# Second layer's attention: 50 joined steps for 80

## The reference

```
s_c = einsum(qc, k_cmp) * scale;  p_c = masked_softmax(s_c, cmp_end <= qpos);  o_c = p_c @ v_cmp    # 31 blocks
s_s = einsum(qr, k_sel) * scale;  p_s = masked_softmax(s_s, tok_pos <= qpos);  o_s = p_s @ v_sel
s_w = einsum(qr, kw_i) * scale;   p_w = masked_softmax(s_w, mask_w);           o_w = p_w @ vw_i
o = gi[..., 0:1] * o_c + gi[..., 1:2] * o_s + gi[..., 2:3] * o_w
```

## Time and profile before

| | |
|---|---|
| median of 3 runs | 3423.38 us (3423.05 to 3425.78) |
| profiled execution | 3428.43 us |
| its span | 3426.1 us |
| PE busy | 3238.9 us |
| DVE, ACT, POOL busy | 1606.8, 1433.4, 1603.5 us |
| second layer's attention, first score phase to the last value phase | 803.54 to 969.23 us |

### The profile page before, as it was taken

How to read it: one execution, slowest core, us unless ns; L and a number is a source line. 1 busy time by engine, 2 the same in 40 slices (tenths; PEclk the granted TensorE clock), 3 DMA queues, 4 the chain that set the end, 5 groups by cost and what they waited for, 6 DMA issues and landing times.

```text
span 3426.1 us, 45293 instructions
## 1 busy us (share of the span) xinstructions
PE 3238.9 (95%) x16790; PEld 2643.6 (77%) x16790; DVE 1606.8 (47%) x2363; ACT 1433.4 (42%) x2565; POOL 1603.5 (47%) x1403
## 2 busy tenths in 40 slices
PE   6789999999999999999989986999999999999998
PEld 4567888876578888788867774888888888888887
DVE  4783443135733431444157875555565562234421
ACT  3355333325753333433245554444454532243332
POOL 4245444655554447444543321444444435554454
PEclk8889999998999999999999997999999999999999
DMA  4111333341013333333321220111111113333332
GB/s 119 50 44 50 98 98 94 97 126 49 2 55 97 94 93 101 88 98 95 97 79 50 62 56 25 32 38 38 38 38 38 44 45 98 98 96 94 98 92 80
DMA packets 471624, 246.88 MB, mean 72 GB/s; under 512 B 13883, under 2 KB 468774, under 8 KB 471334
## 3 DMA queue, kind: packets, MB, share of 16 engines
q1 hardware_dynamic: 470144, 241.33, 24.9%
q10 hardware_dynamic: 1318, 3.35, 0.3%
HBM read 241.51 MB, written 2.10 MB: 71 GB/s over the span
## 4 chain that ended last, share of the span: by engine, by line
PE 84%; DVE 8%; ACT 4%; issue 3%; POOL 1%; DMA 0%; POOLq 0%; ACTq 0%; DVEq 0%
PE ps L466 18%; PE ps L468 18%; PE ps L467 18%; PE ps L2346 2%; PE ps L2242 2%; PE ps L2244 2%; PE ps L2243 2%; PE ps L1573 2%; PE ps L2328 2%; PE ps L1583 2%; PE ps L1596 1%; PE ps L1761 1%; PE ps L1762 1%; PE ps L1763 1%; PE ps L1834 1%
## 5 line engine op out<-in xcount | busy, mean ns | idle before, releaser
L448 POOL TENSOR_TENSOR w_lo<-ring,w_hi 128x512 fp32r<-128x512 f32 (+1 forms) x908 | 1228.1, 1374 | 1543.0 <-ACT w_hi L439 1543.0
L439 ACT ACTIVATE w_hi<-ring 128x512 fp32r<-128x512 f32 (+1 forms) x908 | 516.1, 617 | 1271.6 <-PE ps L468 1199.8
L466 PE MATMUL ps<-h_hi,w_hi 128*128 128x512 f32 x1776 | 701.8, 395 | 4.4 <-POOL w_lo L448 4.4
L468 PE MATMUL ps<-h_hi,w_lo 128*128 128x512 f32 x1776 | 692.6, 390 | 0.0
L467 PE MATMUL ps<-h_lo,w_hi 128*128 128x512 f32 x1640 | 639.3, 390 | 0.0
L466 PEld LDWEIGHTS ps<-h_hi,w_hi 128*128 128x128 f32 x1776 | 334.2, 188 | 81.0 <-POOL w_lo L448 6.4
L468 PEld LDWEIGHTS ps<-h_hi,w_lo 128*128 128x128 f32 x1776 | 333.9, 188 | 69.8
L467 PEld LDWEIGHTS ps<-h_lo,w_hi 128*128 128x128 f32 x1640 | 308.7, 188 | 68.3 <-issue 4.6
L467 PE MATMUL ps<-a_lo,w_hi 128*128 128x512 f32 x752 | 292.6, 389 | 0.0
L466 PE MATMUL ps<-a_hi,w_hi 128*128 128x512 f32 x720 | 280.8, 390 | 0.0
L468 PE MATMUL ps<-a_hi,w_lo 128*128 128x512 f32 x720 | 280.2, 389 | 0.0
(11 more groups left out here) (454 smaller groups left out, 5745.2 us busy)
## 6 DMA issues: line engine op xcount, KB each, us to landing
ring<-in_ffn_w_in SPq DMA_DIRECT2D x176, 512.0 KB, 3.8
ring<-in_w_in SPq DMA_DIRECT2D x96, 512.0 KB, 4.0
ring<-in_ffn_w_down SPq DMA_DIRECT2D x32, 512.0 KB, 3.9
ring<-in_ffn_w_out SPq DMA_DIRECT2D x32, 512.0 KB, 3.8
ring<-in_w_o SPq DMA_DIRECT2D x16, 512.0 KB, 3.9
ring<-in_w_branch_gdn SPq DMA_DIRECT2D x16, 512.0 KB, 3.8
ring<-in_nsa_w_in SPq DMA_DIRECT2D x15, 512.0 KB, 3.9
ring<-in_dsa_w_in SPq DMA_DIRECT2D x13, 512.0 KB, 4.1
```

Source lines behind the costliest of these rows:

```text
L439: act.activation(w_hi[:, (halves(u) + j) % PIECES, 0:n, :], slot(u)[:, j * n:(j + 1) * n, :], ACT.Copy) \
L448: pool.tensor_tensor(w_lo[:, q % PIECES, 0:n, :], slot(u)[:, j * n:(j + 1) * n, :], w_hi[:, q % PIECES, 0:n, :].bitcast(f32), ALU.subtract ...
L466: pe.matmul(dst, wh, hi(k), start=first and k == 0, stop=False)
L468: ins = pe.matmul(dst, wl, hi(k), start=False, stop=last and k == 2 * n - 1)
```

## The change

Units are grouped into steps of one or more segments. In the second layer a pair has seven steps, in this order: (t = 3, br = 1), t = 0 with both wide branches, (2, 1), the blocks (br = 0) of all four token tiles, (3, 2), t = 1 with both wide branches, (2, 2). That is 42 and 8 memory steps: 50. The first layer's steps and the memory steps have one segment and stay as they were.

- Scores: the segments lie side by side in the two banks; the blocks step has eight matmuls of 32 columns, 128 columns per head.
- DVE masks, reduces and sums all segments of a step in one instruction each. For the blocks step it also adds the negated maximum itself, into the ring buffer, so that ACT takes one exponential over both heads and all four tiles; and it multiplies the reciprocals by the gates.
- POOL scales the blocks step with one tensor product against broadcast factors.
- Turning: the blocks step has one 128-column transpose per head. Values: one matmul per head and token tile over all 128 partitions, with a `v_cmp` per token tile that is zero in the rows of the other tiles; the start flag of the accumulation moves to the pair's first step.
- Ahead of attention: the gelu of the value side is written four times, `pe_cmp_second` gives the values on all 128 partitions, and `dve_cmp_values` masks them on DVE where ACT copied them.
- The small tensors have eight columns per step and lie in the former `prT`.

```
+        if i == 1:
+            order = [(3, 1), 0, (2, 1), "blocks", (3, 2), 1, (2, 2)]
...
+    def dve_cmp_values(dve, ch):
+        own = neg_max_raw[:, 0:NT]
+        ch.link(dve.tensor_reduce(own, ident.rearrange("p (i c) -> p i c", i=NT), AX, ALU.add))
+        dve.wait_ge(sig("cmp_done").sem, 1)
+        values = ps[:, 7, 0:2 * HD].rearrange("p (g d) -> p g d", g=2)
+        for g in range(2):
+            ins = dve.tensor_tensor(v_cmp[:, g], values[:, g, :].unsqueeze(1).broadcast_to([P, NT, HD]),
+                                    own.unsqueeze(2).broadcast_to([P, NT, HD]), ALU.mult)
+        ins.then_inc(sig("nsa_copied").sem, 1)
...
 pe_attention
+                for s, seg in enumerate(steps[i]["segs"]):
+                    for hh, (u, rows_) in enumerate(zip(seg, even_odd)):
+                        ins = pe.matmul(ps[:, score_banks(i), s * w:(s + 1) * w][:, hh, :], u["q"][rows_], u["k"][rows_],
+                                        start=True, stop=True)
...
                 for hh in range(2):
+                    for at in range(0, steps[e]["wide"], P):
+                        ins = pe.transpose(ps[:, 2 + hh, at:at + P], p_buf[:, p_slot(e), at:at + P][:, hh, :], ident)
...
+                for s, seg in enumerate(step["segs"]):
+                    for j in range(len(seg[0]["v"])):
+                        at = 0 if step["blocks"] else s * step["w"] + j * P
+                        for hh, u in enumerate(seg):
+                            ins = pe.matmul(ps[even_odd[hh], 4 + pair % 2, u["out"]], u["v"][j],
+                                            prT4[:, 2 * (e % 2) + hh, at:at + P],
...
 dve_attention
+                if step["blocks"]:
+                    raw = neg_max_raw[:, 0:2 * n].rearrange("p (h s) -> p h s", h=2)
+                    ch.link(dve.tensor_reduce(raw, scores, AX, ALU.max, negate=True))
+                    ch.link(dve.tensor_scalar(neg_max[:, columns], neg_max_raw[:, 0:2 * n], -NEG / 10, None, ALU.min))
+                    if i >= DEEP:
+                        dve.wait_ge(sig("att_turned").sem, t["turned"] + i - DEEP + 1)
+                    dve.tensor_tensor(by_seg(p_buf[:, p_slot(i), 0:wide], step), scores,
+                                      top.unsqueeze(3).broadcast_to([P, 2, n, w]), ALU.add) \
                        .then_inc(sig("att_max").sem, 1)
...
+                    ch.link(dve.reciprocal(row_inv[:, before], row_sum[:, before]))
+                    inv = row_inv[:, before].rearrange("p (h s) -> p h s", h=2)
+                    at = 6 * step["pair"]
+                    dve.tensor_tensor(inv, inv, gates[:, :, at:at + 6:3].rearrange("p s h -> p h s"), ALU.mult) \
+                       .then_inc(sig("att_inv").sem, 1)
...
 act_attention
+                if step["blocks"]:
+                    x = p_buf[:, p_slot(i), 0:step["wide"]]
+                    ins = act.activation(x, x, ACT.Exp)
...
 pool_attention
+            if step["blocks"]:
+                x = by_seg(p_buf[:, p_slot(i), 0:step["wide"]], step)
+                inv = row_inv[:, columns_of(i, step)].rearrange("p (h s) -> p h s", h=2)
+                ins = pool.tensor_tensor(x, x, inv.unsqueeze(3).broadcast_to([P, 2, step["n"], w]), ALU.mult)
```

More of the change, by code:

```diff
@@ L322, in build_program @@
     area.take(KT, T)
-    gelu_h = area.take(2, 2, 32)
+    gelu_h = area.take(2, 32)
     swap_area = Area(MEM_AT)
@@ L1489, in build_program, with sum_apart @@
     prT4 = pr
-    def sum_apart(u):
-        return u["nk"] <= P
+    def sum_apart(step):
+        return step["w"] <= P
     def score_banks(i):
@@ L1513, in units_of_layer @@
                                        v=[v_dsa[:, j, at:at + HD] for j in range(t + 1)], gate=None, clamp=False,
-                                       out=tok, first=True, last=True, pair=pair, need=t))
+                                       out=tok, first=True, last=True, pair=pair, need=t, step=t))
                         continue
@@ L1585, in pe_attention @@
[L1585 to L1599, removed]
+                w = steps[i]["w"]
@@ new lines, in pe_attention @@
+            e = i - LAG_V
+            if 0 <= e < S:
+                step = steps[e]
+                pair = step["pair"]
+                pe.wait_ge(sig("att_copied").sem, t["copied"] + e + 1)
+                if pair >= 2 and steps[e - 1]["pair"] != pair:
+                    pe.wait_ge(sig("att_out").sem, t["out"] + pair - 1)
+                begins = layer == 1 and pair < PAIRS and (e == 0 or steps[e - 1]["pair"] != pair)
+                for s, seg in enumerate(step["segs"]):
[4 more added lines that the diff above has]
+                                            prT4[:, 2 * (e % 2) + hh, at:at + P],
+                                            start=(u["first"] or begins and s == 0) and j == 0, stop=u["last"] and j == len(u["v"]) - 1,
+                                            skip_group_check=True)
@@ L1611, in dve_attention @@
             if i < S:
-                u = us[2 * i]
+                step = steps[i]
+                u, n, w, wide = step["segs"][0][0], step["n"], step["w"], step["wide"]
+                columns = columns_of(i, step)
                 if u["need"] > need:
@@ L1616, in dve_attention @@
                 dve.wait_ge(sig("att_scores").sem, t["scores"] + i + 1)
[L1617 to L1622, removed]
+                scores = by_seg(ps[:, score_banks(i), 0:wide], step)
@@ L1629, in dve_attention @@
                        .then_inc(sig("att_max").sem, 1)
                 else:
-                    dve.tensor_reduce(neg_max[:, columns], s, AX, ALU.max, negate=True).then_inc(sig("att_max").sem, 1)
+                    dve.tensor_reduce(top, scores, AX, ALU.max, negate=True).then_inc(sig("att_max").sem, 1)
             if 1 <= i <= S:
-                u, before = us[2 * i - 2], slice(2 * ((i - 1) % DEEP), 2 * ((i - 1) % DEEP) + 2)
+                step = steps[i - 1]
+                before = columns_of(i - 1, step)
```

183 lines of the change are left out of this document (104 added, 79 removed).

## The result

The changed kernel took 3404.48 us as the median of 4 runs (3401.50 to 3406.15) against 3423.44 of 4 runs of the kernel before (3423.05 to 3425.78): a ratio of 0.9942, 95% interval 0.9925 to 0.9959, 19 us less. The forecast was 3397.2 in a range of 3389 to 3410. The forecast of 26.2 us less is a ratio of 0.9923: just outside the first interval and within the second.

A forecast was written before the change was run, and what follows sets the result against it. TensorE (PE), busy 95% of the span, was taken as the bound. Full pairs -21.5, first pair -4.3, clock -1.0 and memory steps +0.6 gave -26.2 us, from 3423.38 to 3397.2, range 3389 to 3410.

The forecast's parts named there:

- Phases: Second layer's attention: seven fuller steps for 12 cost PE 18.49 us per pair, 2.75 less.
- Waits: PE's waits per pair fall from 2.07 to 0.65 us, left only at scores behind the joined t=1 step.
- Start: First attention pair: its 4.6 us excess kept, so 4.3 us less, plus 1.0 less for an earlier clock return.
- Memory steps: The eight memory steps begin with wider work still in the pipe: 0.6 us more.
- Other engines: VectorE, ScalarE and GpSimd stay covered in a pair; GpSimd's product priced at 0.74 us, VectorE's added sum at 0.43.
- rival B: Attention pairs: waits replace saved phases, 20.5 to 21 us per pair, 8 to 12 back, 3405 to 3409; chance 0.16.
- port form: VectorE's clamp, floor and gates product each wait behind a 0.78 us GpSimd scaling: 9 us back, 3406; chance 0.04.
- over 0.3: Sign against the forecast: VectorE's small operations in the blocks step lasting over 0.3 us.
- Ahead of the stage: Compressed values on VectorE and wider gelu before attention: covered, costing nothing; 0.9 us if that cover were gone.
- C: PE doesn't regain 2.4 GHz in the attention stage: pair 33 us, stage about 220, total 3478; chance 0.04.
- D: Attention stage ends earlier but a later load gives the time back; total within 0.2%; chance 0.03.
- The median: Whole kernel: 3402.2 us for the profiled execution, the median of runs 5.05 lower, so 3397.2.

The follow-up runs named there:

- both orders without waits: Changed kernel with only its seven steps reordered: natural order (blocks first) 3397.63 us, ratio 0.9911; order starting (3,1), (3,2) 3399.28 us, ratio 0.9916.
- the doubled maximum: Changed kernel with the row maximum of the joined t=1 step taken twice on VectorE: 3404.07 us in a single run.
- wide-first experiment: Kernel before, 80 steps, with the second layer's token tiles taken from t=3 down to t=0: 3435.48 us, ratio 1.0020.
- dup_blocks: Changed kernel with the row maximum of the blocks step taken three times on VectorE: 3404.55 us in a single run.
- the larger set: Changed kernel repeated without edit: 3405.46 us median of 6 runs against 3428.78 of 17 runs of the kernel before, ratio 0.9928.

## Why the prediction was right, and where not

**Phases.** Worked out as 18.49 us per pair from rows 3; measured 18.46 in both orders without waits, and 19.14 less the 0.68 beyond the usual gap at 843.51, 18.46 again, in the changed kernel. The score phase that no row showed, bounded by 0.75 and 1.06 and taken as 0.99, took 1.01.

**Waits.** One of 0.65 per pair, behind the joined t=1 step: 0.6 measured, at that place, 0.68 by the loads, and the doubled maximum shows that the chain is what makes it. (The chain's terms add up to 5.18, not 5.15, which gives 0.68.) The five full pairs gained 20.9 us for 21.5 forecast.

**Start.** The term that was mis-sized. The first pair was to gain 5.3 us (4.3, and 1.0 for the clock) and gained 9.7, 18.20 for 27.94. The stage, forecast at 139 to 141 us, took 135.96 and 135.08. I took the 20 us at 1.2 GHz of rows 7 as the kernel's own and compared them with the first layer's 13. Two more executions of it showed otherwise: the kernel before had 10 us in its second trace, the changed one about 7 in its first and 3 in its second. The explanation by narrow first steps, on which I counted 1.0 us, has no support in the wide-first experiment. Against before's second trace the first pair gained 5.9 us and the stage 25.9, against its first 9.7 and 29.7; the forecast for the stage was 26.2. So how near the forecast of the stage comes depends on which execution it is held against. That the change shortens the low stretch isn't excluded: over ten traces it lasted 20, 10 and 10 us in the three with 80 steps, 10 with only the blocks joined, and 3 to 7 in the six with seven steps a pair. No run varied that alone.

**Memory steps.** 0.9 longer for 0.6 forecast.

**Other engines.** GpSimd's product took 0.62 us for 0.74 priced. VectorE's sum of scores and maximum took 0.42 for 0.43. The clamp took 0.32 where the trace had shown 0.18 for a narrower one. The three operations of rival B's port form in five full pairs, then the clamp and GpSimd's instructions around it and around the product with the gates, in the changed kernel and, last, in dup_blocks:

```profile
L1671 DVE TENSOR_SCALAR arena<-arena 128x8 f32<-128x8 f32 x5 | 1.6, 320 | 0.2
L1687 DVE TENSOR_SCALAR arena<-arena 128x8 f32<-128x8 f32 x5 | 0.9, 172 | 0.2
L1691 DVE TENSOR_TENSOR arena<-arena 128x8 f32<-128x8 f32 x5 | 0.9, 173 | 0.2
...
852.60 1.73 POOL L1750 TENSOR_SCALAR arena<-arena 128x128 f32<-128x128 f32 x4 [2.11 <-DVE arena L1694]
854.04 0.32 DVE L1671 TENSOR_SCALAR arena<-arena 128x8 f32<-128x8 f32 x1
858.75 0.62 POOL L1745 TENSOR_TENSOR arena<-arena 128x256 f32<-128x256 f32 x1 [2.46 <-DVE arena L1691]
```

```profile
850.52 1.73 POOL L1752 TENSOR_SCALAR arena<-arena 128x128 f32<-128x128 f32 x4 [2.11 <-DVE arena L1696]
852.88 0.17 DVE L1673 TENSOR_SCALAR arena<-arena 128x8 f32<-128x8 f32 x1
853.68 1.31 POOL L1752 TENSOR_SCALAR arena<-arena 128x384 f32<-128x384 f32 x2 [1.43 <-DVE arena L1696]
```

In the changed kernel the clamp starts at 854.04, beside the last of four scalings, and ends with it (854.36 and 854.33). In dup_blocks the doubled reductions put it into a gap of GpSimd, and the same clamp takes 0.17. So its other 0.15 us comes with the scaling beside it, as rival B's port form has it, and not with its width. B priced that at 0.78 for each of three operations. Two of them can't meet a scaling: GpSimd had been idle for 2.46 us, waiting for their result, when it began its product at 858.75. I had named over 0.3 for these as a sign against the forecast. It isn't one: two reductions more in that step cost nothing.

**Ahead of the stage.** Priced at nothing; it cost 0.66 us. The stretch from the first feed-forward part to the start of attention took 496.03 and 496.04 us in the three traces with 80 steps and 496.67 to 496.71 in the seven with joined steps. The step that failed: I asked only whether VectorE and ScalarE are in time and left out PE, which is never idle there. Its weights for the values' second product grew from 31 to 128 columns, and their four loads from 0.25 to 0.53 us. From the first load of the second hidden product to the start of attention it took 10.64 us for 10.37 (795.53 to 806.17 and 793.17 to 803.54), 0.27 of the 0.66. Half of the other 0.4 lies in the first layer's output projection, whose code is the same: from its first weight load, 21 us ahead of this stretch, to the next part's it takes 43.57 to 43.58 us in the three traces with 80 steps and 43.82 to 43.88 in the seven others. Why isn't shown.

**Rivals.** B, waits in place of phases, didn't come, and its port form showed as 0.15 us per pair where it costs PE nothing. C, the clock lost, didn't come in the changed kernel, though it is real: the wide-first kernel lost it in mid-stage. D, the gain given back later, seemed to have come in the first trace (6.9 us in the mixers); over ten traces the mixers take the same with and without joined steps, so that was chance.

**The median.** 19 us less by four runs, 24 by the larger set, 26.2 forecast. Between the two sets the changed kernel hardly moved (3404.48 and 3405.46), the kernel before did (3423.44 and 3428.78). The 5.05 us that the forecast took off, from the profiled execution to the median, was chance of a small set: the median of 17 runs is 0.35 above the profiled execution. The 11.5 us between the two traces of the changed kernel (3404.4 and 3392.9) lie in the second mixer stage, 851 and 839 us for the same instructions at different mean clocks. The runs spread in the same way: of the later six of the changed kernel two took 3393.38 and 3394.70 at a mean granted clock of 0.973 and 0.974, four 3405.14 to 3406.43 at 0.969 to 0.970. In which stage the runs without a trace lost it isn't on record, and what lowers the clock isn't settled; no run varied it. That 3397.2 came within 0.3% of the measured median is in part luck: the stage gained 3.5 us more than forecast, the rest took 8.0 more, and neither was foreseen.

## What to carry to other kernels

When PE is the bound in small dependent phases, count the phases: here each costs about 0.17 us whatever its size, and joining steps with the same matmuls saved 1.80 of the 4.17 us per pair. Then take the longest chain through the other engines and compare it with PE's own phases over the same steps; it tells which single instruction is worth shortening and which may be tripled for nothing. And before a gain of 20 us in 3400 is explained to the last microsecond, profile the same kernel twice and compare its untouched stages first.

## What the runs showed of the hardware that I had not expected

- One kernel's unchanged stage of about 845 us takes 839 to 851 us from one execution to the next, with the same 4791 matmuls at a mean granted clock of 0.96 and 0.94.
- After the idle 3 us at the start of the stage PE ran at 1.2 GHz for 20 us in one execution of the kernel before and for 10 in another.
- Idle times of 0.98 and 1.24 us before weight loads, close together among small phases, were followed by a fall of the clock within the stage in three pairs of five. The same kernel in its own order, where the loads of full pairs wait at most 0.55 for ScalarE, had none in two executions.
- A tensor product on GpSimd with one factor broadcast along the free dimension takes 0.617 us for 128x256, less than the 0.740 of the plain difference in rows 5 (two full operands, fp32r output).
- A clamp of 128x8 on VectorE took 0.32 us where it began beside a scaling on GpSimd and ended with it, and 0.17 where GpSimd was idle.
